# The last two tiles of six down projections in two halves of the tokens

## The chip, the cores and the metric

The kernel runs on one core of a Trainium2 chip. The metric is the device time of one execution in microseconds (us), lower is better. Where the text speaks of TensorE it means the matrix engine; the profile writes PE for its matmuls and PEld for its weight loads. A matmul multiplies a stationary tile of weights (here 128 x 128) with a moving operand of some number of columns (here one column per token) and adds into PSUM.

## The reference, cut to what matters

The reference runs two transformer blocks one after the other on 256 tokens with a model width of 1024. The first has two layers, the second two more on 272 tokens (16 meta tokens are put in front). Six feed-forward networks occur in all, and each ends in a down projection from 2816 hidden values to 1024:

```
def swiglu(h, w_gate, w_up, w_down):
    return (jax.nn.silu(h @ w_gate) * (h @ w_up)) @ w_down
...
def _swiglu(x, wi, wo):
    a, b = jnp.split(x @ wi, 2, axis=-1)
    return (jax.nn.silu(a) * b) @ wo
...
    for layer in range(DEPTH):
        h = h + 0.5 * _swiglu(_rms_norm(h, ln_ffn1[layer]), ffn1_wi[layer], ffn1_wo[layer])
...
        h = h + mix @ w_out[layer]
        h = h + 0.5 * _swiglu(_rms_norm(h, ln_ffn2[layer]), ffn2_wi[layer], ffn2_wo[layer])
    return h[:, N_META:]
```

Between them stand convolution, memory attention, stick-breaking attention, differential attention and a top-k attention. The change does not touch these.

## The kernel before

Everything is kept transposed: features on the 128 partitions, tokens along the columns. Every weight matrix is cut in tiles. Each float32 weight and each activation is split in a high and a low part of the type F32R (`w_hi`, `w_lo`, `act_hi`, `act_lo`), and a product of two is made of three matmuls: high by high, low activation by high weight, high activation by low weight. The helper `product` (line 1866) issues them, lines 1874, 1875 and 1876, one group of three for each 128 x 128 piece of weights; each of the three names its own stationary operand, and each has a weight load of its own in the trace, though the first two use the same one.

A down projection is eight output tiles (`KT = 8`) of 128 features each, and each output tile sums over `FT = 22` pieces. So one tile is 66 matmuls. The number of columns is 256 for the feed-forwards 0, 1 and 5 and 272 for 2, 3 and 4. Tile `d` goes to PSUM bank 4 or 5, in turn, and uses weight slot 0 or 1, in turn. Tile 0 and tile 1 are written out (tile 1 with `heads_first`, lines 1886, 1887 and 1890), tiles 2 to 5 stand in a loop, and tiles 6 and 7 are written out again behind it. The change is in these last two:

```
                for s in range(2):
                    d = KT - 2 + s
                    if s and before_last:
                        before_last()
                    pe.wait_ge(rest_ready, downs.first + d + 1)
                    down(d, s, None)
```

The order of each engine is the order in the code; there is no scheduler. Semaphores tie them: SyncE loads the raw weights of a tile in one of two slots, ScalarE makes `w_hi` (line 804), VectorE (or GpSimd) makes `w_lo`, and `rest_ready` tells TensorE that both are there. `weights_used` goes up at the last matmul of a tile: on it wait VectorE, which adds the bank to the residual `x` (line 1719, then `drained` goes up), and ScalarE, which may then overwrite the slot with the weights two tiles on. `before_last` is given in feed-forward 5 alone: there TensorE turns the first six tiles of the result back (12 transposes, line 1914) between tile 6 and tile 7.

Of the kernel before, what the change touches and what calls it, by code (L numbers as in the profile page):

```python
# [36 lines left out]
FT = F // P  # L37
# [70 lines left out]
def two_blocks(nc, A, out):  # L108
# [6 lines left out]
    def sem(name):  # L115
        return ctx.enter_context(nc.semaphore(name))

    with ctx:
# [93 lines left out]
        bank = ctx.enter_context(nc.psum_tensor("bank", [P, 8, 512], F32))  # L212
# [15 lines left out]
        weights_used, drained = sem("weights_used"), sem("drained")  # L228
# [51 lines left out]
        def width(c):  # L280
            return c.stop - c.start
# [1581 lines left out]
        def _(pe):  # L1863
            mm = pe.matmul

            def product(to, slot, at, moving, cols, order=range(KT), before=None, start=True, stop=True):


                hi, lo = moving
                for i, k in enumerate(order):  # L1870
                    if before:
                        before(i, k)
                    w = slice(at + k * P, at + (k + 1) * P)
                    mm(to, lhsT=w_hi[slot][:, w], rhs=hi[:, k, cols], start=start and i == 0, stop=False)  # L1874
                    mm(to, lhsT=w_hi[slot][:, w], rhs=lo[:, k, cols], start=False, stop=False)  # L1875
                    ins = mm(to, lhsT=w_lo[slot][:, w], rhs=hi[:, k, cols], start=False, stop=stop and i == len(order) - 1)  # L1876
                return ins

            def heads_first(to, slot, at, moving, cols, order, before, lows_ready, start=True, stop=True):

                hi, lo = moving
                for i, k in enumerate(order):
                    if before:
                        before(i, k)
                    w = w_hi[slot][:, at + k * P:at + (k + 1) * P]
                    mm(to, lhsT=w, rhs=hi[:, k, cols], start=start and i == 0, stop=False)  # L1886
                    mm(to, lhsT=w, rhs=lo[:, k, cols], start=False, stop=False)  # L1887
                lows_ready()
                for i, k in enumerate(order):
                    ins = mm(to, lhsT=w_lo[slot][:, at + k * P:at + (k + 1) * P], rhs=hi[:, k, cols], start=False,  # L1890
                             stop=stop and i == len(order) - 1)
                return ins

            def operand(e):

                return lambda i, k: pe.wait_ge(xg_ready, xg_first[e] + k + 1)

            def stats(e):

                c = prep_cols[e]  # L1900
                pe.wait_ge(ssq_ready, summed(e + 1))
                pe.wait_ge(rstd_ready, e)
                mm(stats_bank(e), lhsT=ones[:, :], rhs=ssq[:, c], start=True, stop=True).then_inc(stats_done, 1)

            def input_stats():

                pe.wait_ge(ssq_ready, summed(7))
                pe.wait_ge(rstd_ready, 5)
                mm(stats_bank(5), lhsT=ones[:, :], rhs=ssq[:, REAL], start=True, stop=True).then_inc(stats_done, 1)
                mm(stats_bank(6)[:, 0:META], lhsT=ones[:, :], rhs=meta_ssq, start=True, stop=True)  # L1910
                mm(stats_bank(6)[:, REAL], lhsT=ones[:, :], rhs=gated_ssq, start=True, stop=True).then_inc(stats_done, 1)
# [612 lines left out]
            def feed_forward(f, before_last=None):  # L2524
                ups, downs, n = f.ups, f.downs, width(f.cols)

                late = f.prep not in (6, 9)

                def up(c, s, before=None, between=None):

                    def gate_lows():
                        pe.wait_ge(gate_rest, f.acts + c + 1)

                    def lows_ready():
                        pe.wait_ge(rest_ready, ups.first + c + 1)

                    first = late and isinstance(c, int) and c < 2
                    if first and c:
                        pe.wait_ge(gate_head, f.acts + c + 1)
                    else:  # L2540
                        gate_lows()
                    pe.wait_ge(drained, ups.first + c - 1)

                    pieces = [range(KT)] if before is None else [range(KT - 2), range(KT - 2, KT)]
                    for tiles in pieces:
                        for q in range(2):
                            at = (bank[:, 2 * s + q, 0:n], (ups.first + s) % 2, q * KT * P, xg, f.cols, tiles, before if q == 0 else None)
                            flags = {"start": 0 in tiles, "stop": KT - 1 in tiles}
                            heads = first and q != c and 0 in tiles
                            if q and 0 in tiles:  # L2550
                                if heads:
                                    pe.wait_ge(head_ready, ups.first + c + 1)
                                else:
                                    lows_ready()
                            ins = heads_first(*at, lows_ready if q else gate_lows, **flags) if heads else product(*at, **flags)
                            if q == 0 and KT - 1 in tiles:
                                ins.then_inc(gate_used, 1)
                            if between and q == 0:
                                between()
                    ins.then_inc(weights_used, 1)  # L2560

                if f.prep == 6:
                    up(0, 0, operand(5))
                    input_stats()
                    up(1, 1)
                elif not late:
                    up(0, 0, operand(f.prep))
                    stats(f.prep)
                    up(1, 1)
                else:  # L2570
                    up(0, 0, operand(f.prep))
                    up(1, 1, between=lambda: stats(f.prep))
                with pe.Fori(1, FT // 2) as i:
                    for s in range(2):
                        up(2 * i + s, s)

                def acts_there(i, k):
                    if k in (0, FT - 2):
                        pe.wait_ge(act_ready, f.acts + (FT if k else FT - 2))

                def down(d, s, before):
                    pe.wait_ge(drained, downs.first + d - 1)
                    product(bank[:, 4 + s, 0:n], (downs.first + s) % 2, 0, (f.hi, f.lo), f.act_cols, range(FT), before).then_inc(weights_used, 1)

                def halves_there(i, k):
                    if k == 0:
                        pe.wait_ge(half_rest, f.n + 1)
                    if k == FT // 2:
                        pe.wait_ge(rest_ready, downs.first + 1)
                    acts_there(i, k)  # L2590

                down(0, 0, halves_there)
                pe.wait_ge(head_ready, downs.first + 2)
                pe.wait_ge(drained, downs.first)
                heads_first(bank[:, 5, 0:n], (downs.first + 1) % 2, 0, (f.hi, f.lo), f.act_cols, range(FT), acts_there,
                            lambda: pe.wait_ge(rest_ready, downs.first + 2)).then_inc(weights_used, 1)
                with pe.Fori(1, KT // 2 - 1) as i:
                    for s in range(2):
                        pe.wait_ge(rest_ready, downs.first + 2 * i + s + 1)
                        down(2 * i + s, s, None)  # L2600
                for s in range(2):
                    d = KT - 2 + s
                    if s and before_last:
                        before_last()
                    pe.wait_ge(rest_ready, downs.first + d + 1)
                    down(d, s, None)

            first_mixers(0, 1)
            out_projection(0, EARLY + 1, EARLY + 1, EARLY)
            feed_forward(ffns[0])  # L2610
            first_mixers(1, 3)
            out_projection(1, EARLY + 1, EARLY + 1, EARLY + 1, EARLY + 1)
            feed_forward(ffns[1])
            feed_forward(ffns[2])
            diff_mixer()
            out_projection(2, EARLY + 1, EARLY + 1, EARLY + 1, EARLY + 1, 5)
# [33 lines left out]
```

## Time and profile before

| | |
|---|---|
| time, median of 3 runs | 1666.34 us (1665.48 to 1666.48) |
| span of the profiled execution | 1664.0 us, 2.3 us below the median time (this execution's own time is not given apart from its span) |
| TensorE busy | 1655.3 us, 99% of the span, 13454 matmuls and as many weight loads |
| VectorE, ScalarE, GpSimd busy | 981.6, 863.9 and 604.9 us |
| mean granted TensorE clock | 1.000 |

A matmul's recorded duration contains the time in which it passes through the array, and two to three of them overlap. So durations cannot be added up. What a matmul costs in a dense row of them is the distance between two starts. The weight loads are recorded as an engine of their own, and their starts show that distance best.

### The profile page before, as it was taken

To read this page: it belongs to the slowest core of one execution; us is meant where nothing else is said; L and a number is where in the kernel's file an instruction comes from. 1 tells how busy PE (TensorE), PEld (TensorE's weight loads), DVE (VectorE), ACT (ScalarE), POOL (GpSimd) and SP (SyncE) were. 2 spreads that over 40 slices of the span, in tenths; PEclk is the share of its full clock that TensorE was granted. 3 is DMA by queue.
4 is the path that set the end of the run, shared out by engine and by line. 5 is a ranking of instruction groups with operands and counts; after the bars stand their busy time and mean duration, and the time that the engine had idled before them with its cause. 6 is when DMAs were issued, how large, how long until landed. Compare 5 with 4: busy or idle time off the path is not lost.

```text
span 1664.0 us, 35007 instructions
## 1 busy us (share of the span) xinstructions
PE 1655.3 (99%) x13454; PEld 1625.6 (98%) x13454; DVE 981.6 (59%) x1352; ACT 863.9 (52%) x1322; POOL 604.9 (36%) x489
## 2 busy tenths in 40 slices
PE   9999999999999999999999999999999999999999
PEld 8999999999999999999999999999999998999999
DVE  6785556556655556545567755455555559675543
ACT  7355454455554554443477654444445347765542
POOL 7124334354333543333332233333333525233320
PEclk9999999999999999999999999999999999999999
DMA  9568767553777756666543566666656732366673
GB/s 246 155 169 249 230 191 203 152 140 107 221 230 209 191 159 182 174 180 174 153 122 107 142 187 176 180 174 181 186 173 176 181 90 64 102 180 197 179 198 106
DMA packets 538692, 283.59 MB, mean 170 GB/s; under 512 B 12345, under 2 KB 532912, under 8 KB 538608
## 3 DMA queue, kind: packets, MB, share of 16 engines
q1 hardware_dynamic: 537696, 281.06, 60.9%
q0 software_dynamic: 848, 1.33, 0.4%
q8 instruction: 60, 0.98, 0.3%
q14 instruction: 24, 0.20, 0.0%
q10 hardware_dynamic: 64, 0.02, 0.0%
HBM read 281.29 MB, written 5.53 MB: 172 GB/s over the span
## 4 chain that ended last, share of the span: by engine, by line
PE 94%; DVE 2%; ACT 1%; DMA 1%; SPq 1%; POOL 1%; issue 0%; ACTq 0%; DVEq 0%
PE bank L1874 27%; PE bank L1876 27%; PE bank L1875 27%; PE bank L1887 2%; PE bank L1890 2%; PE bank L1886 2%; PE bank L1914 1%; DMA raw<-in_a_in 1%; PE bank L2411 1%; SPq L433 1%; PE bank L2191 0%; PE bank L2376 0%; ACT w_hi L804 0%; DVE score L1652 0%; PE bank L2024 0%
## 5 line engine op out<-in xcount | busy, mean ns | idle before, releaser
L1874 PE MATMUL bank<-xg_hi,w_hi 128*128 128x256 f32 (+1 forms) x2504 | 717.9, 287 | 0.0
L1876 PE MATMUL bank<-xg_hi,w_lo 128*128 128x256 f32 (+1 forms) x2504 | 714.4, 285 | 0.0
L1875 PE MATMUL bank<-xg_lo,w_hi 128*128 128x256 f32 (+1 forms) x2504 | 712.7, 285 | 0.0
L1874 PEld LDWEIGHTS bank<-xg_hi,w_hi 128*128 128x128 f32 x2504 | 472.2, 189 | 2.1 <-issue 0.7
L1876 PEld LDWEIGHTS bank<-xg_hi,w_lo 128*128 128x128 f32 x2504 | 472.5, 189 | 0.0
L1875 PEld LDWEIGHTS bank<-xg_lo,w_hi 128*128 128x128 f32 x2504 | 471.2, 188 | 0.5
L670 POOL TENSOR_TENSOR up<-gate,up 128x256 f32<-128x256 f32 (+1 forms) x132 | 185.0, 1401 | 397.2 <-ACT gate L1226 396.9
L1313 DVE TENSOR_TENSOR w_lo<-raw,w_hi 128x1024 fp32r<-128x1024 f32 x132 | 161.6, 1224 | 244.3 <-ACT w_hi L813 244.2
L804 ACT ACTIVATE w_hi<-raw 128x2816 fp32r<-128x2816 f32 (+3 forms) x74 | 172.7, 2334 | 194.1 <-PE bank L1876 164.8
L1307 DVE TENSOR_TENSOR w_lo<-raw,w_hi 128x2816 fp32r<-128x2816 f32 (+3 forms) x68 | 196.9, 2895 | 114.1 <-ACT w_hi L804 113.9
L1874 PE MATMUL bank<-act_hi,w_hi 128*128 128x256 f32 (+1 forms) x924 | 263.1, 285 | 0.0
L1875 PE MATMUL bank<-act_lo,w_hi 128*128 128x256 f32 (+1 forms) x924 | 262.8, 284 | 0.0
L1876 PE MATMUL bank<-act_hi,w_lo 128*128 128x256 f32 (+1 forms) x924 | 262.4, 284 | 0.0
L816 ACT ACTIVATE w_hi<-raw 128x1024 fp32r<-128x1024 f32 x132 | 139.6, 1058 | 125.8 <-PE bank L1876 122.2
L606 POOL TENSOR_TENSOR ssq<-ssq,sq 128x272 f32<-128x272 f32 (+1 forms) x56 | 121.4, 2168 | 225.5 <-ACT sq L828 215.7
L1876 PEld LDWEIGHTS bank<-act_hi,w_lo 128*128 128x128 f32 x924 | 173.9, 188 | 0.0
L1875 PEld LDWEIGHTS bank<-act_lo,w_hi 128*128 128x128 f32 x924 | 173.9, 188 | 0.0
L1874 PEld LDWEIGHTS bank<-act_hi,w_hi 128*128 128x128 f32 x924 | 173.7, 188 | 0.0
L1319 DVE TENSOR_TENSOR w_lo<-raw,w_hi 128x1024 fp32r<-128x1024 f32 x131 | 160.1, 1222 | 22.0 <-ACT w_hi L816 22.0
L1228 ACT ACTIVATE act_hi<-up 128x256 f32 (+3 forms) x132 | 56.0, 424 | 221.1 <-POOL up L670 221.1
L813 ACT ACTIVATE w_hi<-raw 128x1024 fp32r<-128x1024 f32 x132 | 138.8, 1051 | 18.1 <-PE bank L1876 17.1
L672 POOL TENSOR_TENSOR act_lo<-up,act_hi 128x256 f32 (+1 forms) x132 | 100.4, 761 | 97.3 <-ACT act_hi L1228 97.3
(394 smaller groups left out, 2351.6 us busy)
## 6 DMA issues: line engine op xcount, KB each, us to landing
raw<-in_ffn_wi SPq DMA_DIRECT2D x176, 512.0 KB, 3.9
raw<-in_ffn_wo SPq DMA_DIRECT2D x32, 1408.0 KB, 7.1
raw<-in_w_gate SPq DMA_DIRECT2D x44, 512.0 KB, 4.0
raw<-in_w_up SPq DMA_DIRECT2D x44, 512.0 KB, 4.8
raw<-in_w_down SPq DMA_DIRECT2D x16, 1408.0 KB, 7.0
raw<-in_a_w_in SPq DMA_DIRECT2D x24, 512.0 KB, 5.3
raw<-in_a_in SPq DMA_DIRECT2D x20, 512.0 KB, 5.8
raw<-in_w_o SPq DMA_DIRECT2D x16, 512.0 KB, 4.8
```

The source lines that it names most:

```text
L606: gp.tensor_tensor(ssq[:, c], ssq[:, c], sq[:, s, c], ALU.add).then_inc(ssq_ready, 1)
L670: gp.tensor_tensor(up, gate, up, ALU.mult).then_inc(act_full, 1)
L672: gp.tensor_tensor(tile(f.lo, c, f.act_cols), up, tile(f.hi, c, f.act_cols).bitcast(F32), ALU.subtract).then_inc(act_ready, 1)
L804: act.activation(w_hi[slot][:, 0:stage.size], raw[slot][:, 0:stage.size], ACT.Copy).then_inc(head_ready, 1)
L813: act.activation(w_hi[slot][:, GATE], raw[slot][:, GATE], ACT.Copy).then_inc(gate_head, 1)
L816: act.activation(w_hi[slot][:, UP], raw[slot][:, UP], ACT.Copy).then_inc(head_ready, 1)
L1307: v.tensor_tensor(w_lo[slot][:, 0:n], raw[slot][:, 0:n], w_hi[slot][:, 0:n].bitcast(F32), ALU.subtract).then_inc(rest_ready, 1)
L1313: v.tensor_tensor(w_lo[slot][:, GATE], raw[slot][:, GATE], w_hi[slot][:, GATE].bitcast(F32), ALU.subtract).then_inc(gate_rest, 1)
L1319: v.tensor_tensor(w_lo[slot][:, UP], raw[slot][:, UP], w_hi[slot][:, UP].bitcast(F32), ALU.subtract).then_inc(rest_ready, 1)
L1874: mm(to, lhsT=w_hi[slot][:, w], rhs=hi[:, k, cols], start=start and i == 0, stop=False)
L1875: mm(to, lhsT=w_hi[slot][:, w], rhs=lo[:, k, cols], start=False, stop=False)
L1876: ins = mm(to, lhsT=w_lo[slot][:, w], rhs=hi[:, k, cols], start=False, stop=stop and i == len(order) - 1)
```

## The change

```
@@ feed_forward, in the TensorE program
                     if s and before_last:
                         before_last()
                     pe.wait_ge(rest_ready, downs.first + d + 1)
-                    down(d, s, None)
+                    pe.wait_ge(drained, downs.first + d - 1)
+                    for q in range(2):
+                        part, acts = (slice(c + q * n // 2, c + (q + 1) * n // 2) for c in (0, f.act_cols.start))
+                        ins = product(bank[:, 4 + s, part], (downs.first + s) % 2, 0, (f.hi, f.lo), acts, range(FT))
+                    ins.then_inc(weights_used, 1)
```

Tile 6 and tile 7 of every down projection are computed in two passes. The first takes the first half of the tokens, the second the other half, into the two halves of the same bank. A half is 128 columns where there were 256, and 136 where there were 272. Each pass goes through all 22 pieces, so every weight piece is named again in the second pass. The wait on `drained` is the one that stood in `down`. `weights_used` goes up once, at the end of the second pass.

In TensorE's program at the first of these places, feed-forward 0, the rows where tile 6 ends and tile 7 begins read so before (`w_hi0` and `w_hi1` are the two weight slots):

```order
L1874 MATMUL bank<-act1_hi,w_hi0 128x256
L1875 MATMUL bank<-act1_lo,w_hi0 128x256
L1876 MATMUL bank<-act1_hi,w_lo0 128x256
L1874 MATMUL bank<-act1_hi,w_hi1 128x256
L1875 MATMUL bank<-act1_lo,w_hi1 128x256
L1876 MATMUL bank<-act1_hi,w_lo1 128x256
```

The slot changes after 66 rows. In the changed program the same place reads as follows.

```order
L1874 MATMUL bank<-act1_hi,w_hi0 128x128
L1875 MATMUL bank<-act1_lo,w_hi0 128x128
L1876 MATMUL bank<-act1_hi,w_lo0 128x128
L1874 MATMUL bank<-act1_hi,w_hi1 128x128
L1875 MATMUL bank<-act1_lo,w_hi1 128x128
L1876 MATMUL bank<-act1_hi,w_lo1 128x128
```

The slot now changes after 132 rows, and each row has half the columns. Where tile 7 ends and the next stage begins (`mg` is the normalised memory), the changed program has these rows:

```order
L1874 MATMUL bank<-act1_hi,w_hi1 128x128
L1875 MATMUL bank<-act1_lo,w_hi1 128x128
L1876 MATMUL bank<-act1_hi,w_lo1 128x128
L1874 MATMUL bank<-mg_hi,w_hi0 128x256
L1875 MATMUL bank<-mg_lo,w_hi0 128x256
L1876 MATMUL bank<-mg_hi,w_lo0 128x256
```

Behind the tile nothing has moved: the next stage keeps its own shape and its order. TensorE's program grows from 6660 rows to 7452, that is by 792; VectorE's, ScalarE's and SyncE's are the same row for row.

## Rows read from the trace of the kernel before

**Rows 1.** The page, engines: busy us (share of the span) and instructions.

```profile
PE 1655.3 (99%) x13454; PEld 1625.6 (98%) x13454; DVE 981.6 (59%) x1352; ACT 863.9 (52%) x1322; POOL 604.9 (36%) x489
```

**Rows 2.** The page, 40 slices: TensorE's busy share and its granted clock.

```profile
PE   9999999999999999999999999999999999999999
...
PEclk9999999999999999999999999999999999999999
```

**Rows 3.** The page, chain of work that ended last, by engine.

```profile
PE 94%; DVE 2%; ACT 1%; DMA 1%; SPq 1%; POOL 1%; issue 0%; ACTq 0%; DVEq 0%
```

**Rows 4.** Waits of TensorE: us in total, times, longest us.

```profile
PE bank L1914 <- POOL ident L572: 2.3, 1, 2.3
PE bank L1914 <- DMA memin<-in_mem: 0.7, 1, 0.7
PE bank L1914 <- DVE apd L1591: 0.6, 1, 0.6
...
PE bank L1914 <- DVE x L1719: 0.3, 1, 0.3
```

**Rows 5.** Groups by form on TensorE: busy us, mean ns of one.

```profile
L1874 PE MATMUL bank<-act_hi,w_hi 128*128 128x272 f32 x462 | 133.1, 288 | 0.0
L1874 PE MATMUL bank<-act_hi,w_hi 128*128 128x256 f32 x462 | 129.9, 281 | 0.0
L2026 PE MATMUL bank<-spl_hi,ones_r 128*128 128x128 f32 x12 | 2.0, 249 | 0.0
```

**Rows 6.** Weight loads, timeline, feed-forward 0: first of tile 6, first behind tile 7.

```profile
285.42 0.19 PEld L1874 LDWEIGHTS bank<-act_hi,w_hi 128*128 128x128 f32 x1
...
301.09 0.19 PEld L1874 LDWEIGHTS bank<-mg_hi,w_hi 128*128 128x128 f32 x1
```

**Rows 7.** Weight loads, timeline, feed-forward 2: first of tile 6, first behind tile 7.

```profile
791.86 0.19 PEld L1874 LDWEIGHTS bank<-act_hi,w_hi 128*128 128x128 f32 x1
...
808.36 0.19 PEld L1874 LDWEIGHTS bank<-xg_hi,w_hi 128*128 128x128 f32 x1
```

**Rows 8.** Weight loads, timeline, feed-forward 5: transposes, tile 7, transposes.

```profile
1650.57 1.33 PEld L1914 LDWEIGHTS bank<-ident,x 128*128 128x128 f32 x12
...
1651.87 0.19 PEld L1874 LDWEIGHTS bank<-act_hi,w_hi 128*128 128x128 f32 x1
...
1659.67 0.24 PEld L1914 LDWEIGHTS bank<-ident,x 128*128 128x128 f32 x2
```

**Rows 9.** Weight loads, timeline, a stretch of the top-k attention with narrow matmuls.

```profile
1405.87 0.30 PEld L2376 LDWEIGHTS bank<-kk,raw 128*128 128x128 f32 x2 [0.17 <-issue]
1406.10 0.31 PEld L2385 LDWEIGHTS bank<-ones,qs 128*128 128x128 f32 x2
1406.34 0.30 PEld L2376 LDWEIGHTS bank<-kk,raw 128*128 128x128 f32 x2
1406.57 0.31 PEld L2385 LDWEIGHTS bank<-ones,qs 128*128 128x128 f32 x2
1406.80 0.19 PEld L2372 LDWEIGHTS bank<-kk_hi,w_hi 128*128 128x128 f32 x1
```

**Rows 10.** The matmuls of the stretch of rows 9.

```profile
1406.22 0.28 PE L2385 MATMUL bank<-ones,qs 128*128 128x1 f32 x2
1406.36 0.49 PE L2376 MATMUL bank<-kk,raw 128*128 128x144 f32 x2
```

**Rows 11.** Weight loads, timeline, stick-breaking attention: F32R with 128 columns (L2026).

```profile
341.87 0.36 PEld L2026 LDWEIGHTS bank<-spl_lo,ones_r 128*128 128x128 f32 x2
342.16 0.19 PEld L1874 LDWEIGHTS bank<-kv_hi,w_hi 128*128 128x128 f32 x1
342.27 0.19 PEld L1875 LDWEIGHTS bank<-kv_lo,w_hi 128*128 128x128 f32 x1
342.39 0.19 PEld L1876 LDWEIGHTS bank<-kv_hi,w_lo 128*128 128x128 f32 x1
```

**Rows 12.** The matmuls of the stretch of rows 11.

```profile
342.05 0.34 PE L2026 MATMUL bank<-spl_lo,ones_r 128*128 128x128 f32 x2
342.22 0.33 PE L1874 MATMUL bank<-kv_hi,w_hi 128*128 128x256 f32 x1
```

**Rows 13.** Weight loads, timeline, the first transposes of the program.

```profile
2.30 2.64 PEld L1914 LDWEIGHTS bank<-ident 128*128 128x128 f32 x13 [2.30 <-POOL ident L572]
```

## The prediction

> **What bounds the kernel now.** I read the page's engine line first: TensorE is busy 99% of the span, the next engine 59% [rows 1]. The slices say that this holds everywhere, and that the granted clock is at its upper level all along [rows 2]. The chain that ended last lies on TensorE for 94% [rows 3]. TensorE's waits are next: the longest kinds are 2.3 us and 0.7 us, both at the start of the program, and the only one behind a down tile is 0.3 us at the very end [rows 4]. So there is no idle time near the changed tiles that could take up a longer stretch of matmuls. What TensorE gains or loses there the span gains or loses in full.
>
> What does one matmul cost in a dense row? Not its duration (281 and 288 ns for 256 and 272 columns [rows 5]), for these overlap. I take the distance of starts over a long run, from the weight loads. Tiles 6 and 7 of feed-forward 0 run from 285.42 to 301.09 us: 15.67 us for 132 matmuls of 256 columns, 118.7 ns each [rows 6]. In feed-forward 2 they run from 791.86 to 808.36: 16.50 us for 132 of 272 columns, 125.0 ns each [rows 7]. Tile 7 of feed-forward 5 takes 1659.67 - 1651.87 = 7.80 us for 66 [rows 8], so a pair there is 15.60. I count 15.65 us for a pair of tiles with 256 columns.
>
> At the granted clock of 2.4 GHz 256 columns are 106.7 ns and 272 are 113.3. What is left over is 12 ns in both, so it belongs to the instruction and not to the column. That sixteen columns more cost 6.3 ns (16 / 2.4 = 6.7) says that these matmuls are paced by their columns, just about. It does not say how far down that goes.
>
> **What the change removes and adds.** Removed are 12 tiles of 66 matmuls, 792 in all: three pairs of 256 columns and three of 272, 3 x 15.65 + 3 x 16.50 = 96.5 us. Added are 12 tiles of 132, 1584 matmuls with 128 or 136 columns. The columns in total are the same. The number of matmuls and, with it, of weight loads is up by 792: the trace has as many loads as matmuls, 13454 each [rows 1], though line 1875 uses the weights that line 1874 has just loaded. A repeated stationary operand is loaded again here.
>
> **The price of a narrow one** is the open term. The question is whether its own weight load, which runs beside the matmul ahead of it, is shorter than 128 columns (53.3 ns at 2.4 GHz). The best place for that is the top-k attention, where pairs of loads alternate between matmuls of 144 columns and of 1 column [rows 9, 10]. Eight loads fill 1405.87 to 1406.80, 116 ns each. The loads of L2385 feed one-column matmuls: from 1406.10 the next group begins at 1406.34, two loads in 240 ns; and the two of L2376 behind them, the first of which has only a one-column matmul beside it, take 230. A matmul of one column has nothing to stream, so this is the pace of the loads. That is 115 to 120 ns a load. The only row of the changed tiles' own type with 128 columns is L2026. Its two loads stand 0.36 - 0.19 = 0.17 us apart, the second held by a matmul of 384 columns; from there, 342.04, the next ones follow at 342.16, 342.27 and 342.39 [rows 11], 110 to 120 ns apart. The load at 342.27 has a 128-column matmul behind it and is no earlier for that.
>
> So a load of 128 x 128 in this type needs 110 to 117 ns beside whatever runs, the same as the 256-column matmul takes, and two or three times what 128 columns need. Both 128 and 136 columns fall below it, so both get one price. I take 116 ns, the mean of the eight loads [rows 9], because that is the longest row of loads with narrow matmuls between. The bounds: not below 108, the pace of the 12 transposes, (1651.87 - 1650.57) / 12 [rows 8], whose loads are not shorter in elements and which move 128 columns; not above 120, two loads in 240 ns [rows 9].
>
> A changed pair of tiles is then 264 x 0.116 = 30.6 us. That is 15.0 us more for 256 columns and 14.1 us more for 272. **The sum:** 3 x 15.0 + 3 x 14.1 = 87.3 us. With 108 ns a pair is 28.5 us and the sum 3 x 12.9 + 3 x 12.0 = 74.6. With 120 it is 31.7 and 3 x 16.0 + 3 x 15.2 = 93.6. The span goes from 1664.0 to about 1751. Nothing around the span changes, so I add 87.3 to the median of 1666.34: 1753.6 us. The bounds give 1741 and 1760.
>
> What I cost at nothing: the wait on `drained` stood in `down` already. Another 792 instructions on TensorE's queue are in their pairs' price. VectorE adds tile 6 and 7 to `x` as late behind them as before, since `weights_used` goes up at the end of the second pass: what waits for it (that addition, and the cast of the next weights on ScalarE) shifts with TensorE. Between these points the other engines only get more time, some 15 us in each of six places, which nothing uses, for TensorE waits for no one there [rows 4].
>
> The Trainium skill (TensorE: Matmul & The Clock Gate, section Back-to-back issue gap) has another price for this: a sustained stream of load and matmul pairs runs at about 81 ns each for 128 columns and 131 ns for 512. By that figure, as an estimate, a changed pair is 264 x 0.081 = 21.4 us, and the sum some 32 us, for 1698. The trace is at 116 ns where loads pace it, and the same page (section Weight-path perf modes) says that its fast weight load is not on for FP32, which would go with a slower load here.
>
> **The rivals.** First, *half-hidden loads*. Two F32R matmuls of 128 columns start at 342.05, and what is behind them at 342.22, 85 ns each [rows 12]. If that were the pace, a pair of tiles is 264 x 0.085 = 22.4 us, and the sum 3 x 6.8 + 3 x 5.9 = 38.1: 1704. This is the row version of the page's 81 ns. Against it: the 256-column matmul at 342.22 is recorded with 0.33 us in place of 0.28, so it stood 50 ns waiting for its load, which began only at 342.16 [rows 11, 12]. Starts of two are too short a run. 7%.
>
> Second, *the columns pace it*. If a load were hidden even beside 128 columns, a matmul would cost 53.3 + 12 = 65 ns, or 56.7 + 12 = 69 with 136. A pair is 17.2 or 18.2 us, and the sum 3 x 1.5 + 3 x 1.7 = 9.6: 1676. The one-column rows speak against it (115 to 120 ns in place of some 12). 4%.
>
> Third, *the clock falls*. In the changed tiles the array works 53 of 116 ns, for 30 us at a stretch, where now it works 107 of 119. The trace has no such long stretch; in those it has, of some 1 to 3 us, the clock stays up [rows 2, 9]. The 13 transposes at the start of the program, behind 2.3 us of nothing, run at (2.64 - 0.19) / 12 = 204 ns against 108 at the end [rows 8, 13], so a slow array would about double the price, at 1.2 GHz. If it fell for half of each pair, 6 tiles at 15.3 us more: 87 + 92, 1845. 6%. The Trainium skill (TensorE: Matmul & The Clock Gate, section The HAM clock gate) has 1.2 GHz for an array that has not been busy, by which it would be this rival; no row here shows the clock falling.
>
> Fourth, the other side, *not slower*: the second use of the same weights needs no load, and the 12 ns belong to the load. Then 1584 matmuls cost their columns alone, 3 x 264 x 53.3 and 3 x 264 x 56.7 ns, 87.1 us in place of 96.5, for 1657. It decides when a load costs nothing beyond the columns, so at a pace below 61 ns. The count of loads, and the 65 other matmuls that stand between the two uses of a piece, speak against it. 1%.
>
> **How the numbers follow.** Loads pace it 82%, half-hidden 7%, clock 6%, columns 4%, not slower 1%. The likeliest gives 1753.6, with its own bounds 1741 to 1760. The first case holds more than 8 in 10, so the range stays with it, with 2 us either way for the run to run difference and rounding: 1739 to 1762. A difference of 0.2%, 3.3 us, is about what a measurement of this kernel can tell. All cases but the last are above that: slower 0.98, same 0.01, faster 0.01.
>
> **What would show it.** Right: TensorE has 792 more matmuls and as many more loads; in the changed tiles the loads stand 108 to 120 ns apart with 128 and with 136 columns alike; a pair takes about 30.6 us in feed-forward 0 as in 2; the granted clock stays at 1.0; everywhere else the pitch and the waits are as before. Wrong: loads 85 ns or 65 ns apart, a pair in feed-forward 2 longer than one in 0, a lower clock in those slices, or TensorE idle in front of the next stage.

## The result, and the profile after

The changed kernel takes 1746.49 us (median of 4 runs, 1746.10 to 1746.93) against 1666.17 us for the kernel before on the same chip. The ratio is 1.0482 with a 95% interval of 1.0469 to 1.0494: 80.3 us slower. The forecast was 1753.6 us with a range of 1739 to 1762.

The page of the changed kernel has the same picture as [rows 1, 2] with 792 more matmuls and 792 more loads:

```profile
span 1744.7 us, 36591 instructions
...
PE 1736.4 (100%) x14246; PEld 1706.9 (98%) x14246; DVE 981.7 (56%) x1352; ACT 863.7 (50%) x1322; POOL 604.1 (35%) x489
...
PEclk9999999999999999999999999999999999999999
```

The other engines are as busy as before, to the microsecond. The granted clock has not moved. So the 80.7 us more of span must stand on TensorE. Its waits do not hold them either; three of the rows read:

```profile
PE bank L1914 <- POOL ident L572: 2.3, 1, 2.3
PE bank L2056 <- DVE mg_lo L1330: 0.8, 1, 0.8
PE bank L1914 <- DVE apd L1591: 0.6, 1, 0.6
```

The one new row is the second. It is 0.8 us long and lies at 10 us, far ahead of the first changed tile, and the wait of 0.7 us for `memin` near it [rows 4] is gone in exchange: TensorE's waits add up to 4.6 us in both kernels. What others wait for did grow: VectorE's addition to `x` (line 1719) waits 153.9 us in all on TensorE where it waited 73.6, since it now stands by while TensorE works longer.

The weight loads (timeline: start, duration, engine, line) of tiles 6 and 7 show where it is. Feed-forward 0, which answers to [rows 6]:

```profile
285.59 0.19 PEld L1874 LDWEIGHTS bank<-act_hi,w_hi 128*128 128x128 f32 x1
...
314.63 0.19 PEld L1876 LDWEIGHTS bank<-act_hi,w_lo 128*128 128x128 f32 x1
314.74 0.19 PEld L1874 LDWEIGHTS bank<-act_hi,w_hi 128*128 128x128 f32 x1
314.85 0.19 PEld L1875 LDWEIGHTS bank<-act_lo,w_hi 128*128 128x128 f32 x1
314.96 0.19 PEld L1876 LDWEIGHTS bank<-act_hi,w_lo 128*128 128x128 f32 x1
315.07 0.19 PEld L1874 LDWEIGHTS bank<-mg_hi,w_hi 128*128 128x128 f32 x1
```

and feed-forward 2, which answers to [rows 7]:

```profile
819.75 0.19 PEld L1874 LDWEIGHTS bank<-act_hi,w_hi 128*128 128x128 f32 x1
...
849.24 0.19 PEld L1874 LDWEIGHTS bank<-xg_hi,w_hi 128*128 128x128 f32 x1
```

Both pairs of tiles take the same time: 29.48 and 29.49 us for 264 loads, 111.7 ns each, with 128 columns as with 136. Before they took 15.67 and 16.50. The sum over all six is 3 x 13.8 + 3 x 13.0 = 80.4 us, which is the whole result but for 0.3 us, and 0.2 us of these lie ahead of the first changed tile (it begins at 285.59, before at 285.42). The 0.11 us from row to row at the end of the first fence can be read off directly.

### The profile page after: what moved, and what is told of

Read it like the earlier page. It is cut to its first block, busy times and chain, and to the rows that moved or that the text cites. A ratio compares the mean times of both kernels' runs of the same rounds, so it can differ in the third digit from the quotient of the medians.

```text
span 1744.7 us, 36591 instructions
## 1 busy us (share of the span) xinstructions
PE 1736.4 (100%) x14246; PEld 1706.9 (98%) x14246; DVE 981.7 (56%) x1352; ACT 863.7 (50%) x1322; POOL 604.1 (35%) x489
## 4 chain that ended last, share of the span: by engine, by line
PE 95%; ACT 2%; DVE 2%; POOL 1%; issue 0%; DMA 0%; SPq 0%; ACTq 0%; POOLq 0%; DVEq 0%
PE bank L1874 28%; PE bank L1876 27%; PE bank L1875 27%; PE bank L1887 2%; PE bank L1890 2%; PE bank L1886 2%; PE bank L1914 2%; PE bank L2411 1%; PE bank L2191 0%; PE bank L2376 0%; DMA raw<-in_a_in 0%; ACT w_hi L804 0%; PE bank L2024 0%; DVE score L1652 0%; PE bank L2337 0%
## 5 line engine op out<-in xcount | busy, mean ns | idle before, releaser
L1874 PE MATMUL bank<-act_hi,w_hi 128*128 128x272 f32 (+3 forms) x1188 | 333.1, 280 | 0.0
L1875 PE MATMUL bank<-act_lo,w_hi 128*128 128x272 f32 (+3 forms) x1188 | 332.7, 280 | 0.0
L1876 PE MATMUL bank<-act_hi,w_lo 128*128 128x272 f32 (+3 forms) x1188 | 332.7, 280 | 0.0
L1876 PEld LDWEIGHTS bank<-act_hi,w_lo 128*128 128x128 f32 x1188 | 225.6, 190 | 0.0
L1875 PEld LDWEIGHTS bank<-act_lo,w_hi 128*128 128x128 f32 x1188 | 225.6, 190 | 0.0
L1874 PEld LDWEIGHTS bank<-act_hi,w_hi 128*128 128x128 f32 x1188 | 225.4, 190 | 0.0
```

## The experiments

All but the last start from the changed kernel and touch only tiles 6 and 7 of the six down projections. Theory A is the prediction's: a narrow matmul costs the length of its weight load. Theory B: it costs a fixed part and its columns. Theory C: a pair of load and matmul has a price of its own, whatever the size of either. One half, widths, narrow weights and loads of 96 leave part of these tiles out of the computation, and bf16 computes them less precisely. One half and joined were timed in 4 and 11 executions, the others in one each; the kernel before, timed beside them, took 1665.55 to 1666.38 us (medians).

**One half.** The second pass is gone.

```
-                    for q in range(2):
+                    for q in range(1):
```

> The changed kernel without the second pass of tiles 6 and 7: one pass of 66 matmuls of 128 or 136 columns, so half the tokens of these tiles are left out of the computation. In the changed kernel's trace a matmul of either width costs 111.7 ns. Theory A, the weight loads pace narrow matmuls: a pair of tiles is 132 x 0.1117 = 14.74 us, against 15.65 (256 columns) and 16.50 (272) before the change, so half the columns save only 3 x 0.91 + 3 x 1.76 = 8.0 us: 1658 us. Theory B, a matmul costs its columns and a fixed part of about 58 ns: the same 111.7 for 128 columns, so the same time here; it is told apart by the widths run. Theory D, narrow matmuls cost their columns (65 and 69 ns) and the changed kernel lost its time elsewhere: 8.6 and 9.1 us a pair, 43 us saved, 1623 us.

Measured: 1658.17 us, ratio to the kernel before 0.9955 (0.9938 to 0.9971). With half of their columns gone, twelve tiles give back 8 us of some 96. Theory A's number was 1658; theory D, that the time had been lost elsewhere, is out. Theory B is not, for it gives the same price at 128 columns.

**Widths.** One pass, with another number of columns in each feed-forward.

```
...
+                    wide = (192, 224, 240, 264, 16, 2)[f.n]
+                    ins = product(bank[:, 4 + s, 0:wide], (downs.first + s) % 2, 0, (f.hi, f.lo), slice(0, wide), range(FT))
...
```

> Tiles 6 and 7 as before the change, one pass of 66 matmuls, but over 192, 224, 240, 264, 16 and 2 of the columns in feed-forwards 0 to 5; the other tokens are left out. Read is the distance of weight loads in each. Theory A: 112 ns at 2, 16, 192 and 224 columns, 112 at 240 (240 / 2.4 + 12), 122 at 264, a flat floor and then a slope of 1 column per 0.417 ns. Theory B, a fixed 58 ns and the columns: 59, 65, 138 and more, a slope from the start. The total under A is 1666.2 less 3 x 0.9 + 2 x 1.75 + 0.3, about 1660 us.

Measured: 1682.1 us. The stretches view (busy us and number in each window, then the granted clock) has these rows for 192, 224 and 264 columns, and one from inside the tiles with 16:

```profile
286.00:300.00 14.00, 14.00 (x128) 14.00 (x126) 8.42 (x6) 7.54 (x8) 6.11 (x2) 1.00 0.84 223
592.00:606.00 14.00, 14.00 (x127) 14.00 (x126) 8.07 (x7) 6.78 (x9) 6.78 (x5) 1.00 0.68 191
...
1122.00:1138.00 16.00, 16.00 (x134) 16.00 (x133) 8.20 (x7) 6.04 (x7) 4.96 (x2) 1.00 0.65 185
```

```profile
1340.00:1346.00 6.00, 6.00 (x30) 6.00 (x29) 0.00 (x0) 0.00 (x0) 0.00 (x0) 0.50 0.28 86
```

The two counts behind the first busy times are matmuls and loads (x126 loads in 14 us is 111 ns). 192 and 224 columns cost the same as 128: a floor. Averaged over both tiles the distances are 111.7 ns for 192 and for 224, 112.3 for 240 and 121.2 for 264. That is theory A's flat floor with a slope behind it, and B is out. The total missed by 22 us, though, for a reason that A does not have: with 16 and with 2 columns the granted clock fell to 0.50 within the tiles, 4.0 and 4.4 us after they had begun. Up to the fall the loads stand 0.11 us apart with these columns too, behind it 213 ns. The two pairs took 24.5 and 24.3 us in place of 14.7, and that is 19 of the 22 us; the last fence shows the slow stretch.

**Quarters.** Four passes of 64 or 68 columns.

```
-                    for q in range(2):
-                        part, acts = (slice(c + q * n // 2, c + (q + 1) * n // 2) for c in (0, f.act_cols.start))
+                    for q in range(4):
+                        part, acts = (slice(c + q * n // 4, c + (q + 1) * n // 4) for c in (0, f.act_cols.start))
```

> The whole computation, tiles 6 and 7 in four passes of 64 or 68 columns, 264 matmuls a tile. Theory A, the loads pace: 111.7 ns each as with halves, a pair of tiles 59.0 us, 29.5 more than with halves, six times 177 us over 1746: 1923 us. Theory B, columns (27 to 28 ns) and a fixed 58: 85 ns each, a pair 44.9, 1839 us. The granted clock may fall, since the array streams only 27 of 112 ns; if it stays at 1.0 the clock rival of the prediction is out.

Measured: 2227.8 us, far above both. The stretches at feed-forward 0, where tile 6 begins at 285.6:

```profile
280.00:285.40 5.40, 5.40 (x48) 5.40 (x47) 4.36 (x3) 1.75 (x4) 3.26 (x1) 1.00 0.51 125
285.40:288.00 2.60, 2.60 (x27) 2.60 (x25) 0.42 (x1) 2.07 (x1) 0.00 (x0) 1.00 1.05 307
288.00:290.00 2.00, 2.00 (x21) 2.00 (x20) 1.49 (x1) 1.58 (x4) 1.14 (x1) 1.00 1.20 294
290.00:292.00 2.00, 2.00 (x18) 2.00 (x18) 2.00 (x2) 0.00 (x0) 2.00 (x1) 0.88 0.27 64
292.00:294.00 2.00, 2.00 (x12) 2.00 (x11) 0.86 (x2) 0.00 (x0) 0.19 (x1) 0.50 0.46 130
294.00:300.00 6.00, 6.00 (x30) 6.00 (x30) 0.00 (x0) 0.00 (x0) 0.00 (x0) 0.50 0.83 219
```

and the loads of the same kernel around the fall:

```profile
291.20 0.19 PEld L1876 LDWEIGHTS bank<-act_hi,w_lo 128*128 128x128 f32 x1
291.31 0.19 PEld L1874 LDWEIGHTS bank<-act_hi,w_hi 128*128 128x128 f32 x1
291.42 0.23 PEld L1875 LDWEIGHTS bank<-act_lo,w_hi 128*128 128x128 f32 x1
291.53 0.34 PEld L1876 LDWEIGHTS bank<-act_hi,w_lo 128*128 128x128 f32 x1
291.75 0.33 PEld L1874 LDWEIGHTS bank<-act_hi,w_hi 128*128 128x128 f32 x1
291.96 0.33 PEld L1875 LDWEIGHTS bank<-act_lo,w_hi 128*128 128x128 f32 x1
```

For the first 5.9 us a matmul of 64 columns costs 0.11 us, the same as one of 128: A's floor, where B has 85 ns. At 291.5 the clock goes from 2.4 to 1.2 GHz and the distance to 213.3 ns (from 292.18 on, without exception). 213.3 ns is 256 cycles at 1.2 GHz, and 111.7 ns is 256 cycles at 2.4 GHz and 5 ns. That fits a load of 128 x 128 in F32R that takes two array cycles a column, at either clock. At 213.3 ns a pair is 112.6 us and the total would be 1923 + 6 x 53.6 = 2245; the measured 2227.8 has the first 3.5 to 5.9 us of each of the six pairs at full clock, and, the other way, the first 3.2 to 5.5 us of the next stage at the lower one. TensorE had no gap before the clock fell; what it did in those microseconds was stream 64 columns in every 111.7 ns. The Trainium skill (TensorE: Matmul & The Clock Gate, section The HAM clock gate) lists these two levels in its table of states, and the trace agrees (0.50 and 1.00).

**Narrow weights.** The halves stay, each weight piece is loaded in two loads of 64 columns.

```
...
+                        for r in range(2):
...
+                                    ins = mm(bank[0:HD, 4 + s, part],
+                                             lhsT=wt[slot][:, k * P + r * HD:k * P + (r + 1) * HD], rhs=act[:, k, part],
...
```

> Tiles 6 and 7 with the halves of the change, and each weight piece in two loads of 64 of its columns: 264 matmuls a tile, 128 x 64 stationary, 128 or 136 columns moving. Both weight halves are added into the same 64 rows of the bank, so what is computed of these tiles isn't the down projection. Theory A, the load's own length paces, in proportion to its columns: a load is then some 58 ns, and the matmul's columns with 12 ns on top pace instead, 65 and 69 ns: 528 x 0.067 = 35.4 us for a pair against 29.5, 1782 us. Theory C, any pair of load and matmul costs 112 ns whatever the size of the load: 59.0 a pair, 1923 us.

Measured: 1766.5 us. Feed-forwards 0 and 2:

```profile
287.00:317.00 30.00, 30.00 (x503) 30.00 (x502) 9.42 (x7) 6.42 (x8) 6.86 (x2) 1.00 0.54 141
827.00:857.00 30.00, 30.00 (x472) 30.00 (x470) 8.75 (x5) 4.29 (x6) 6.91 (x2) 1.00 0.48 122
```

Twice as many instructions as the change has, at 60 and 64 ns each. Theory C (112 ns a pair of instructions) is out. And here, for the first time, 136 columns cost more than 128: the load has become short enough for the columns to show. A's estimate of 65 and 69 ns was 5 ns high, and its total of 1782 us was 16 us high with it.

**Loads of 96.** As many loads and matmuls as in the change, each load with 96 of its 128 columns.

```
...
+                                ins = mm(bank[0:96, 4 + s, part], lhsT=wt[slot][:, k * P:k * P + 96], rhs=act[:, k, part],
...
```

> The changed kernel with 96 of the 128 weight columns in each matmul of tiles 6 and 7; the number of matmuls and of loads, 132 a tile, and their 128 or 136 moving columns stay. A quarter of the rows of these tiles is left out of the computation. Theory A, the load's length paces, two array cycles for each of its columns and 5 ns (111.7 ns for 128, and at most 60 for 64, as the run with loads of 64 columns showed): 96 / 1.2 + 5 = 85 ns, a pair 22.4 us against 29.5, 1746.5 - 6 x 7.1 = 1704 us, with no difference between 128 and 136 moving columns. If a load of more than 64 columns had the full price, 1746 us.

Measured: 1705.17 us, and in feed-forwards 0 and 2:

```profile
287.00:308.00 21.00, 21.00 (x250) 21.00 (x249) 9.79 (x8) 7.34 (x8) 6.87 (x2) 1.00 0.63 171
807.00:828.00 21.00, 21.00 (x250) 21.00 (x249) 9.19 (x6) 6.69 (x6) 6.91 (x2) 1.00 0.65 171
```

249 loads in 21 us are 84 to 85 ns, with 128 and with 136 moving columns alike: 96 / 1.2 + 5, so 85. The moving side is as in the change, only the stationary operand is a quarter narrower, and half of the loss (41 of 80 us) is gone. That is the cause shown by its size: the price follows the stationary columns.

A matmul with fewer stationary columns also yields fewer rows, and no run parts its own time from that of its load. The recorded lengths of the loads speak for the load (from 287 to 300 us of the changed kernel, of loads of 96 and of narrow weights; ns, shortest/median/longest):

```profile
L1876 PEld LDWEIGHTS bank<-act_hi,w_lo x40: 192/192/192, 286.8 to 299.9; 128*128 128x128 f32 x40
...
L2612 PEld LDWEIGHTS bank<-act_hi,w_lo x52: 165/165/165, 286.9 to 299.9; 128*96 128x96 f32 x52
...
L2613 PEld LDWEIGHTS bank<-act_hi,w_lo x73: 134/134/136, 287.0 to 300.0; 128*64 128x64 f32 x73
```

From 64 to 128 columns a load grows by 58 ns, 0.9 ns a column, near the two cycles (0.83 ns) that the distances give.

**bf16.** The same halves with the upper two bytes of each operand.

```
...
+                                ins = mm(bank[:, 4 + s, part], lhsT=wt[slot][:, k * P:(k + 1) * P].bitcast(b16)[:, 1::2],
+                                         rhs=act[:, k, part].bitcast(b16)[:, 1::2],
...
```

> Tiles 6 and 7 with the halves of the change, but both operands read as bf16, the upper two bytes of each value, every second element: 132 matmuls a tile, same columns and same number of loads, lower precision. Theory A, the load of this type is slow, twice its 128 columns at 2.4 GHz: with bf16 the load may be as short as 53 ns and the pitch 60 to 81 ns (the Trainium skill, TensorE: Matmul & The Clock Gate, section Back-to-back issue gap, has 81), a pair 17 to 21 us, 1671 to 1697 us. If the load of 128 columns costs 107 ns in every type, the pitch stays at 112 and the time at 1746 us.

Measured: 1664.32 us. Feed-forward 0, and feed-forward 2:

```profile
286.00:300.00 14.00, 14.00 (x249) 14.00 (x249) 8.72 (x7) 7.53 (x8) 6.41 (x2) 1.00 0.83 216
792.00:807.00 15.00, 15.00 (x245) 15.00 (x243) 8.74 (x5) 6.06 (x6) 6.89 (x2) 1.00 0.69 175
```

The pitch is 56.7 ns with 128 columns and 62 with 136: the load is out of sight, and twice as many matmuls cost no more than the whole ones did. The Trainium skill (TensorE: Matmul & The Clock Gate, section Back-to-back issue gap) has 81 ns for sustained pairs of this size; the trace is below it, and the time is below my bracket (1671 to 1697). So the loss belongs to the type F32R and not to narrow matmuls as such.

**Same weights twice.** Both halves of a matmul next to each other.

```
...
+                            for q in range(1 if whole else 2):
...
+                                ins = mm(bank[:, 4 + s, part], lhsT=wt[slot][:, k * P:(k + 1) * P], rhs=act[:, k, part],
...
```

> The whole computation, tiles 6 and 7 in halves, but both halves of a matmul next to each other, so that two in a row use the same weights (the first and the last matmul of a tile are whole: 130 a tile). Theory A, each matmul has its load whether or not the weights are in place: 111.7 ns, 29.1 us a pair, 1744 us. If a repeated stationary operand were cheaper to load: between 65 and 112 ns, down to 17.4 us a pair and 1674 us.

Measured: 1746.06 us. The matmuls are recorded in twos, and their loads too:

```profile
309.88 0.30 PEld L2613 LDWEIGHTS bank<-act_hi,w_hi 128*128 128x128 f32 x2
310.11 0.30 PEld L2613 LDWEIGHTS bank<-act_lo,w_hi 128*128 128x128 f32 x2
310.33 0.30 PEld L2613 LDWEIGHTS bank<-act_hi,w_lo 128*128 128x128 f32 x2
```

Two loads in 0.22 to 0.23 us. That a matmul names the weights that the one ahead of it has just used saves nothing.

**Uneven.** Passes of 192 and 64 (or 80) columns.

```
...
+                    for part in (slice(0, 192), slice(192, n)):
+                        ins = product(bank[:, 4 + s, part], (downs.first + s) % 2, 0, (f.hi, f.lo), part, range(FT))
...
```

> The whole computation, tiles 6 and 7 in two passes of 192 and 64 columns (192 and 80 where there are 272). Theory A: both passes are under the length of the load, so both cost 111.7 ns a matmul and the time is that of equal halves, 1746.5 us, as long as the granted clock stays up. With passes of 64 columns throughout the clock fell about 6 us after they began, and the load then took 213 ns; a pass of 66 matmuls of 64 columns is 7.4 us, so it could fall near its end: up to some 1 to 4 us more for each of six to twelve passes, 1750 to 1780 us.

Measured: 1798.84 us, above the upper figure of 1780. The first pass of 64 columns begins at 294.1 in feed-forward 0, and the stretches there read:

```profile
294.00:296.00 2.00, 2.00 (x21) 2.00 (x20) 0.00 (x0) 0.00 (x0) 0.00 (x0) 1.00 0.79 231
296.00:300.00 4.00, 4.00 (x30) 4.00 (x30) 0.00 (x0) 0.00 (x0) 0.00 (x0) 0.76 1.03 273
300.00:302.00 2.00, 2.00 (x12) 2.00 (x11) 0.00 (x0) 0.00 (x0) 0.00 (x0) 0.50 0.00 0
302.00:308.00 6.00, 6.00 (x29) 6.00 (x30) 0.81 (x2) 3.18 (x3) 0.00 (x0) 0.50 0.00 0
```

Up to the fall both widths run at 0.11 us, as A has it. Then the clock is down from 298.1 to 308.3 us. The narrow pass ends at 304.5, so nearly 4 us of the next pass of 192 run slow. In the second narrow pass it falls again, and stays low from 318.6 to 328.8 us, while tile 7 ends at 323.3. I had counted only the end of the narrow pass as slow.

**Joined.** From the kernel before, in feed-forwards 0, 1 and 5: high and low activations as one moving operand of 512.

```
...
+                def highs(k):
+                    mm(bank[:, b, 0:2 * SEQ], lhsT=w_hi[slot][:, k * P:(k + 1) * P], rhs=f.both[:, :, k, 0:SEQ], start=k == 0, stop=False)
...
+                def lows(k):
+                    return mm(bank[:, b, 0:SEQ], lhsT=w_lo[slot][:, k * P:(k + 1) * P], rhs=f.both[:, 0, k, 0:SEQ], start=False, stop=k == FT - 1)
...
```

> The kernel before, and in the three down projections with 256 tokens the matmuls of the high weights take high and low activations in one moving operand of 512 columns, into the two halves of a bank; VectorE adds both halves to x. The whole computation. A piece is two matmuls and two loads in place of three. If a matmul costs its columns and 12 ns, a piece is 225 + 119 = 344 ns in place of 355.5, 11.7 ns less: 22 x 8 x 3 x 0.0117 = 6.2 us, less some 0.5 us for the added step of VectorE at the end: 1660.5 us. If the 12 ns were a cost of the columns, or of the load and hidden beside 512, no change: 1666 us.

Measured: 1664.69 us against 1666.38, ratio 0.999 (0.9981 to 0.9999): 1.7 us less, within 0.2% of no change, and neither of the two forecasts. Tiles 6 and 7 of feed-forward 0:

```profile
285.17 0.19 PEld L1906 LDWEIGHTS bank<-act,w_hi 128*128 128x128 f32 x1
285.29 0.19 PEld L1909 LDWEIGHTS bank<-act,w_lo 128*128 128x128 f32 x1
...
300.62 0.19 PEld L1883 LDWEIGHTS bank<-mg_hi,w_hi 128*128 128x128 f32 x1
```

15.45 us for 44 pieces, 351 ns a piece against 356: less 118.7 for its matmul of 256 columns, the one of 512 costs 233 ns, 19 more than its columns at 2.4 GHz. So the 12 ns that I had read in [rows 6, 7] as a price of the instruction are for the most part a price of the columns. Only 5 of the hoped-for 11.7 ns a piece are there, 2.5 us in all, and at the end TensorE waits 0.8 us for VectorE where it waited 0.3.

## Why the prediction was right

- *TensorE bounds the kernel and nothing near the tiles takes up the time.* Right: 80.4 us longer tiles are the 80.7 us of span but for 0.3 us. No wait of TensorE appeared behind a changed tile.
- *A repeated operand is loaded again.* Right, by the count of loads (14246) and by the run with the same weights twice.
- *The load paces matmuls of 128 and 136 columns alike.* Right: 111.7 ns for both, shown as its cause by the loads of 96 columns (85 ns) and of 64 (60 and 64 ns, now paced by the moving columns).
- *The price, 116 ns.* This is the term that was mis-sized: 111.7 measured, 1584 x 4.3 ns = 6.8 us of the 7 us between 87.3 and 80.3. I took the eight loads of the top-k attention [rows 9], of another operand type and between other matmuls, since theirs was the longest row. The three distances of the one F32R stretch [rows 11] were 0.12, 0.11 and 0.12, not precise enough to choose by, though the middle one was nearer. The lower bound of 108 held in part by luck: the transposes behind it [rows 8] have loads of 138 to 144 ns where those of `act_hi,w_hi` have 188, so their pace was not that of the changed tiles' loads.
- *12 ns of every matmul belong to the instruction.* This reading failed, though nothing in the sum hung on it. The distances measured where columns pace are 60 ns (128), 64 (136), 118.7 (256), 121.2 (264), 125 (272) and 233 (512): about 0.45 ns a column and 2 to 3 ns fixed, not 0.417 and 12. The column rival's 65 and 69 ns were too high by 5 for the same reason.
- *The rival half-hidden loads* (85 ns) is out: the single starts behind [rows 12] are 342.045, 342.106 and 342.217, so its 85 ns was the mean of 61 and 111, and every long row gives 111.7. With it goes, for F32R, the 81 ns that the prediction took from the Trainium skill (TensorE: Matmul & The Clock Gate, section Back-to-back issue gap); by it the time would be 1698 us. *The rival on the clock* did not happen with 128 columns, but its mechanism is real: it decided the time of quarters and of uneven, and the miss of widths. Its price, 1.9 times, was right as well (213.3 against 111.7).

## What to carry to other kernels

Before you cut a matmul in two, compare its columns with its weight load: in F32R the load of 128 columns costs 112 ns here, so anything under some 240 moving columns is paid at that floor, and the kernel before stood just above it (119 ns at 256). Read the floor from starts of weight loads of the same operand type, and doubt a price that comes from two starts. Where passes get much narrower than the load, look at the granted clock before anything else, since its fall nearly doubled the price here and lasted on into the next, wide pass.

## What the runs showed of the hardware

- A load of a 128-row F32R operand costs two array cycles a column, and at 2.4 GHz about 5 ns more: 111.7 ns for 128 columns and 85 for 96, and 213.3 ns for 128 at 1.2 GHz. With bf16 it is hidden beside a 56.7 ns matmul.
- F32R columns stream at about 0.45 ns each, and 2 to 3 ns a matmul (60 ns at 128, 125 at 272, 233 at 512), where 2.4 GHz would be 0.417. I have no cause for the difference.
- In bf16, 136 columns cost 62 ns and 128 cost 56.7, more than eight columns' worth. This stays open.
- TensorE's clock can fall without a gap in its instructions: with 64 or 68 columns a load it fell 3.5 to 5.9 us after each of the six pairs of tiles had begun (in the first at 291.5 against 285.6), with 128 or 136 it stayed at 1.00 through twelve tiles of 14.7 us. In uneven it came back at 308.3, 3.9 us after the pass of 192 columns had begun.
